# First panel by halves behind X's first tile with 19 zero products ahead; other orders at both attentions' ends and in the last network

## What is computed

```
h = rms_norm(x, g_attn); z = h @ w_in
o_fox = fox_attention(...)                 # 8 heads of 64, causal, with forget gates
o_nsa = nsa_attention(...)                 # 8 heads of 64: compressed, selected and window branches
merged = sigmoid(g_a) * (o_fox @ w_br_fox) + sigmoid(g_b) * (o_nsa @ w_br_nsa)
x = x + merged @ w_out
x = x + square(relu(rms_norm(x, g_mlp) @ w_ff1)) @ w_ff2
x = rms_norm(x, g_final)
...                                        # second block: modulation from c, context keys and values
hx = modulate(rms_norm(x, norm1_g), sh1, sc1)
mix = (sigmoid(g_a) * (attn @ w_attn_out) + sigmoid(g_b) * conformer_conv(u)) @ w_out
x = x + g1 * mix
hx2 = modulate(rms_norm(x, norm2_g), sh2, sc2)
a, b = split(hx2 @ w_up); x = x + g2 * ((gelu(depthwise_conv(a)) * b) @ w_down)
return rms_norm(x, final_g)
```

## Time and profile before

| | |
|---|---|
| median of 3 runs | 1682.06 us (1680.8 to 1686.5) |
| profiled execution, its own time | 1686.16 us |
| its span (first to last instruction) | 1684.4 us |
| PE busy | 1621.0 us (96%) |
| DVE busy | 1110.1 us (66%) |
| ACT busy | 716.3 us (43%) |
| mean granted clock of TensorE | 0.992 |

### The profile page before, as it was taken

The page is one execution under the profiler, slowest core; times in us unless marked ns, Lnnn a source line. Parts: engine busy times, 40 slices in busy tenths (PEclk is TensorE's granted clock), DMA queues, the critical chain, the costliest instruction groups (busy, mean ns, idle before and its releaser), DMA issues.

```text
span 1684.4 us, 21985 instructions
## 1 busy us (share of the span) xinstructions
PE 1621.0 (96%) x7956; PEld 1338.8 (79%) x7956; DVE 1110.1 (66%) x1700; ACT 716.3 (43%) x1236; POOL 164.6 (10%) x188
## 2 busy tenths in 40 slices
PE   7999989989999999999999999999999999999997
PEld 5887777767888888888877787888779888888886
DVE  6666787786676666753686579998765644444446
ACT  5446775665443232322443234545633432232233
POOL 0121200000310000000003970000000000000000
PEclk9999999999999999999999999999999999999999
DMA  4566511112625555532213222221333223322333
GB/s 162 163 180 180 119 47 51 51 59 63 248 89 212 186 191 189 195 125 76 88 63 125 88 63 63 47 61 51 110 109 89 84 92 100 100 93 94 100 100 101
DMA packets 50001, 185.45 MB, mean 110 GB/s; under 512 B 6952, under 2 KB 9256, under 8 KB 47488
## 3 DMA queue, kind: packets, MB, share of 16 engines
q1 hardware_dynamic: 39600, 136.76, 25.6%
q0 software_dynamic: 10320, 47.62, 9.1%
HBM read 174.85 MB, written 6.87 MB: 108 GB/s over the span
## 4 chain that ended last, share of the span: by engine, by line
PE 82%; DVE 10%; ACT 4%; issue 3%; DMA 1%; SPq 0%; ACTq 0%; DVEq 0%
PE ps L2045 18%; PE ps L2047 17%; PE ps L2046 17%; PE ps L2107 2%; PE ps L2109 2%; PE ps L2108 2%; PE ps L2289 1%; PE ps L2454 1%; PE ps L2456 1%; PE ps L2455 1%; PE ps L2291 1%; PE ps L2290 1%; PE ps L2250 1%; PE ps L2511 1%; PE ps L2275 1%
## 5 line engine op out<-in xcount | busy, mean ns | idle before, releaser
L2045 PE MATMUL ps<-h_hi,w_hi 128*128 128x512 f32 x832 | 329.1, 396 | 8.4 <-DVE h_lo L1705 3.7
L2047 PE MATMUL ps<-h_hi,w_lo 128*128 128x512 f32 x832 | 324.0, 389 | 0.0
L2046 PE MATMUL ps<-h_lo,w_hi 128*128 128x512 f32 x832 | 323.9, 389 | 0.0
L1198 DVE TENSOR_TENSOR w_lo<-raw,w_hi 128x1024 fp32r<-128x1024 f32 x181 | 227.6, 1260 | 103.3 <-ACT w_hi L683 77.7
L616 ACT ACTIVATE w_hi<-raw 128x1024 fp32r<-128x1024 f32 x125 | 131.4, 1052 | 166.7 <-DMA raw<-in_panels 166.6
L2045 PEld LDWEIGHTS ps<-h_hi,w_hi 128*128 128x128 f32 x832 | 156.2, 188 | 48.6 <-DVE h_lo L1705 5.8
L2046 PEld LDWEIGHTS ps<-h_lo,w_hi 128*128 128x128 f32 x832 | 156.2, 188 | 33.6 <-issue 1.9
L2047 PEld LDWEIGHTS ps<-h_hi,w_lo 128*128 128x128 f32 x832 | 156.2, 188 | 32.8
L2045 PE MATMUL ps<-f_hi,w_hi 128*128 128x512 f32 x408 | 164.8, 404 | 0.0
L2046 PE MATMUL ps<-f_lo,w_hi 128*128 128x512 f32 x408 | 159.1, 390 | 0.0
L2047 PE MATMUL ps<-f_hi,w_lo 128*128 128x512 f32 x408 | 159.0, 390 | 0.0
(11 more groups left out here) (426 smaller groups left out, 3333.8 us busy)
## 6 DMA issues: line engine op xcount, KB each, us to landing
raw<-in_panels SPq DMA_DIRECT2D x252, 512.0 KB, 3.5
wm<-in_w_mod POOLq DMA_DIRECT2D x16, 1536.0 KB, 8.2
scratch_r<-scratch_t POOLq DMA_DIRECT2D x8, 320.0 KB, 5.3
kd<-k_hi POOLq DMA_DIRECT2D x16, 128.0 KB, 2.6
kd<-k_lo POOLq DMA_DIRECT2D x16, 128.0 KB, 3.3
bias<-scratch_c POOLq DMA_DIRECT2D x8, 256.0 KB, 3.8
bias<-scratch_r POOLq DMA_DIRECT2D x8, 256.0 KB, 3.0
X<-in_x POOLq DMA_DIRECT2D x1, 2048.0 KB, 9.4
```

The lines of the kernel that those rows point to most:

```text
L1198: dve.tensor_tensor(w_lo[:, n % RING], raw[:, n % RING], w_hi[:, n % RING].bitcast(F32), ALU.subtract)\
L2045: pe.matmul(out, w_hi[:, u, b, :], hi[:, k, :N], start=start, stop=False)
L2046: pe.matmul(out, w_hi[:, u, b, :], lo[:, k, :N], start=False, stop=False)
L2047: ins = pe.matmul(out, w_lo[:, u, b, :], hi[:, k, :N], start=False, stop=stop)
```

## The change

1. Start: X's first tile is issued first, then the 8 columns of the vectors that the first norm needs, then panel 0 in two halves of four blocks around X's second tile; the constants come behind panel 1 and the other vectors behind panel 2. ACT and DVE split panel 0 by halves. TensorE begins when the first halves and two tiles of `h_lo` are there. Ahead of it TensorE multiplies a zero tile by itself 19 times into a bank that is not read.
2. `LAST_GATE` names other slots for four gate pieces.
3. `column_sum("norm2", T)` stands ahead of `ctx_part(1)`.
4. Second attention: in steps 14 and later ACT copies part 2 ahead of the exponentials; DVE moves `o2_lo` of head 6 and a tap behind two low parts.
5. Last network: the high and low parts of `up_0`'s panels 1 and 3 come earlier, and the second half's column sum is done in the middle of panel 1.

The semaphore of one table transfer is also merged into `rows_stored`, whose thresholds rise by 16.

```diff
-    LAST_GATE = ((NI - 1, 0), (NI, 2), (NI + 1, 2), (NI + 1, 3))
+    LAST_GATE = ((NI, 2), (NI, 5), (NI + 1, 0), (NI + 1, 2))
...
-        sp.dma_start(vec[:], a["vectors"]).then_inc(in_v, 16)
         for n, (f, g) in enumerate(X_PARTS):
             sp.dma_start(X[:, f:g, :], a["x"][:, f:g, :]).then_inc(in_x[n], 16)
             if n == 0:
-                sp.dma_start(raw[:, 0], a["panels"][0]).then_inc(landed[0], 16)
+                sp.dma_start(vec[:, 0:KT], a["vectors"][:, 0:KT]).then_inc(in_x[0], 16)
+                sp.dma_start(raw[:, 0, 0:4, :], a["panels"][0][:, 0:4, :]).then_inc(sem("first_half_landed"), 16)
+            if n == 1:
+                sp.dma_start(raw[:, 0, 4:8, :], a["panels"][0][:, 4:8, :]).then_inc(landed[0], 16)
+        sp.dma_start(raw[:, 1], a["panels"][1]).then_inc(landed[1], 16)
         sp.dma_start(cst[:, 0:C_EARLY], a["consts"][:, 0:C_EARLY]).then_inc(in_c, 16)
...
# ScalarE, the start
             if f == 0:
-                first_hi(0)
+                act.wait_ge(sem("first_half_landed"), 16)
+                act.activation(w_hi[:, 0, 0:4, :], raw[:, 0, 0:4, :], ACT.Copy)
+            if f == 1:
+                act.wait_ge(landed[0], 16)
+                act.activation(w_hi[:, 0, 4:8, :], raw[:, 0, 4:8, :], ACT.Copy).then_inc(hi_ready, 1)
...
# ScalarE, second attention and last network
-            exp2(w, 0)
-            hi_turn2(w - 1, 2)
+            if w >= UNITS - 2:
+                hi_turn2(w - 1, 2)
+                exp2(w, 0)
+            else:
+                exp2(w, 0)
+                hi_turn2(w - 1, 2)
...
+        panel_hi(BASE["up_0"] + 1)
         second_square("out2", "norm_ffn", 6)
-        panel_hi(BASE["up_0"] + 1)
...
# VectorE, second attention
-            taps_at(w, 0)
+            taps_at(w, 0) if w < UNITS else None
             lo_turn2(w - 1, 0)
             lo_turn2(w - 1, 1)
+            if w == UNITS:
+                o2_lo(H2 - 2)
+                taps_at(w, 0)
...
-            if w >= 3 and w % 2:
+            if w >= 3 and w % 2 and w != UNITS - 1:
                 o2_lo((w - 3) // 2)
...
# VectorE, last network
         ffn_low(0, 6)
+        panel_lo(BASE["up_0"] + 1)
         ffn_low(0, 7)
...
-        panel_lo(BASE["up_0"] + 1)
+        panel_lo(BASE["up_0"] + 2)
         inverse("norm_ffn", 1)
-        panel_lo(BASE["up_0"] + 2)
+        panel_lo(BASE["up_0"] + 3)
...
         for f in range(1, KT):
-            if f == 2:
-                panel_lo(BASE["up_0"] + 3)
...
# TensorE
-            pe.wait_ge(lo_ready, n + 1)
+            pe.wait_ge(lo_ready, n + 1) if n else None
...
-                    pe.wait_ge(n_lo, k + 1)
+                    pe.wait_ge(n_lo, max(k, 1) + 1)
+                if n == 0 and k == 4:
+                    pe.wait_ge(lo_ready, 1)
...
+        pe.wait_ge(setup, 1)
+        zeros = p_cmp[0][:].rearrange("p t c -> p (t c)")
+        for n in range(19):
+            pe.matmul(ps[:, 7, 0:P], zeros, zeros, start=True, stop=True)
...
         ctx_part(0)
+        column_sum("norm2", T)
         ctx_part(1)
-        column_sum("norm2", T)
...
-            half_panel(BASE["up_0"] + m, m, 0, ready=(lambda k: (n_lo, 24 + k + 1)) if m == 0 else None)
-            half_sum("norm_ffn", 1) if m == 0 else None
+            half_panel(BASE["up_0"] + m, m, 0, ready=(lambda k: (n_lo, 24 + k + 1)) if m == 0 else None,
+                       at_four=(lambda: half_sum("norm_ffn", 1)) if m == 1 else None)
```

More of the change, by code:

```diff
@@ L468, in _ @@
             if n == 0:
-                sp.dma_start(raw[:, 0], a["panels"][0]).then_inc(landed[0], 16)
+                sp.dma_start(vec[:, 0:KT], a["vectors"][:, 0:KT]).then_inc(in_x[0], 16)
[3 more added lines that the diff above has]
+        sp.dma_start(raw[:, 1], a["panels"][1]).then_inc(landed[1], 16)
         sp.dma_start(cst[:, 0:C_EARLY], a["consts"][:, 0:C_EARLY]).then_inc(in_c, 16)
-        for u in range(1, RING):
-            sp.dma_start(raw[:, u], a["panels"][u]).then_inc(landed[u], 16)
+        sp.dma_start(raw[:, 2], a["panels"][2]).then_inc(landed[2], 16)
+        sp.dma_start(vec[:, KT:V_ALL], a["vectors"][:, KT:V_ALL]).then_inc(in_v, 16)
+        sp.dma_start(raw[:, 3], a["panels"][3]).then_inc(landed[3], 16)
         if total > RING:
@@ L494, in _ @@
         gp.wait_ge(sem("rel_rows"), 2)
-        gp.dma_start(scratch_t, r8[:]).then_inc(sem("rel_placed"), 16)
-        gp.wait_ge(sem("rel_placed"), 16)
+        gp.dma_start(scratch_t, r8[:]).then_inc(sem("rows_stored"), 16)
+        gp.wait_ge(sem("rows_stored"), 16)
         for n in range(8):
@@ L537, in _ @@
         gp.dma_start(w2v[:], a["w2v"]).then_inc(sem("w2_loaded"), 16)
-        gp.wait_ge(sem("rows_stored"), 16)
+        gp.wait_ge(sem("rows_stored"), 32)
         bias_rows(0)
@@ L595, in _ @@
             gp.dma_start(scratch_f[h], factor[:, h % 2, :]).then_inc(sem("rows_stored"), 16)
-            gp.wait_ge(sem("rows_stored"), 16 * (h + 2))
+            gp.wait_ge(sem("rows_stored"), 16 * (h + 3))
             gp.wait_ge(sem("factor_loaded"), 16 * h) if h else None
@@ L701, in _ @@
         act.activation(row_max[:, 0, 0:1], p_cmp[0][:, 0, 0:1], ACT.Copy)
-        act.wait_ge(in_v, 16)
         for f in range(KT):
-            act.wait_ge(in_x[X_PART_OF[f]], 16)
+            act.wait_ge(in_x[X_PART_OF[f]], 16 if f else 32)
             act.activation(h_hi[:, f, :], X[:, f, :], ACT.Copy, scale=vcol("g_attn", f)).then_inc(n_hi, 1)
             if f == 0:
-                first_hi(0)
+                act.wait_ge(sem("first_half_landed"), 16)
[3 more added lines that the diff above has]
+                act.activation(w_hi[:, 0, 4:8, :], raw[:, 0, 4:8, :], ACT.Copy).then_inc(hi_ready, 1)
         first_hi(1)
@@ L715, in _ @@
         act.wait_ge(in_c, 16)
+        act.wait_ge(in_v, 16)
         act.activation(row_max[:, 0, 0:1], eps, ACT.Sqrt)
@@ L1206, in _ @@
         dve.memset(blk_f[:].rearrange("p j (g c) -> p (j g) c", c=CW)[:, :, NCB:CW], 0.0).then_inc(setup, 1)
-        dve.wait_ge(in_v, 16)
+        dve.wait_ge(in_x[0], 32)
         for f in range(KT):
             dve.wait_ge(n_hi, f + 1)
+            if f == 1:
+                dve.tensor_tensor(w_lo[:, 0, 0:4, :], raw[:, 0, 0:4, :], w_hi[:, 0, 0:4, :].bitcast(F32), ALU.subtract)
             dve.scalar_tensor_tensor(h_lo[:, f, :], X[:, f, :], vcol("g_attn", f), h_hi[:, f, :].bitcast(F32),
                                      ALU.mult, ALU.subtract).then_inc(n_lo, 1)
-            if f == 0:
-                panel_lo(0)
+            if f == 1:
+                dve.wait_ge(hi_ready, 1)
+                dve.tensor_tensor(w_lo[:, 0, 4:8, :], raw[:, 0, 4:8, :], w_hi[:, 0, 4:8, :].bitcast(F32), ALU.subtract)\
+                   .then_inc(lo_ready, 1)
         panel_lo(1)
@@ L1224, in _ @@
         panel_lo(3)
+        dve.wait_ge(in_v, 16)
         dve.wait_ge(n_rms, 1)
@@ L1820, in factor2_of @@
             dve.wait_ge(sem("exp2_done"), 2 * (w + 1))
-            dve.wait_ge(sem("rows_stored"), 16 * h) if h >= 2 else None
+            dve.wait_ge(sem("rows_stored"), 16 * (h + 1)) if h >= 2 else None
             dve.reciprocal(factor[:, h % 2, :], row_sum[:, h % 2, :]).then_inc(sem("o_factor"), 1)
```

## The result

The changed kernel takes 1674.95 us (median of 8 executions, 1672.59 to 1678.14); the kernel before took 1683.89 us in its 8 executions beside them (1680.8 to 1686.5). The ratio is 0.9949, with a 95% interval of 0.9938 to 0.9960: 8.6 us faster by the ratio, 8.9 by the two medians. Forecast were 1672.5 in a range of 1668 to 1680, and "faster" with 0.77. The profiled execution took 1677.28 us (span 1675.5, mean granted clock 0.992), 8.9 less than that of before.

The account below looks back on a forecast made before the run. TensorE's stream plus its waits and slow stretches bound the kernel. -2.8 + 0.3 - 1.6 - 4.0 - 3.1 = -11.2; with 1.6 taken off for clock, 9.6 below 1682.06 is 1672.5 us, range 1668 to 1680.

Parts of the forecast that it names:

- Start: Up to panel 1's first product: TensorE begins it at 15.4 instead of 18.25, a gain of 2.8 us.
- the bound of 15: At the start, worst case: the zero products end near 15 us and the start loses 3.
- First attention's end: Moving gate pieces around the last unit's turns costs 0.3 us; bounds: gain of 0.8, loss of 1.5.
- Norm 2: Column sum moved ahead: TensorE waits 0.6 for it, the reciprocal starts at 853.6 instead of 855.22; gain 1.6 us.
- Second attention's end: Reordering on DVE (1.3 us) and ACT (1.1) shortens TensorE's wait, and the clock stays up (1.6); gain 4.0 in sum.
- the third: Second attention's end: with a shorter wait the clock should not fall, giving back 1.7 us, counted as 1.6.
- rival E: Inside the two attentions, short waits bring the clock down more often; 1.7 us per stretch, 1689.5 with ten; chance 0.04.
- Last network: Panel 1's products fill the column sum's wait and the last `h_lo` ends earlier; `up_0`'s second round gains 3.1 us.
- new stretches: Sign against the prediction: the clock shows new stretches at 0.50 inside the attentions.
- 1.6 off for clock in a lump: Whole kernel: 1.6 us of the gain taken off for stretches at 0.50 that a median run did not have.
- rivals B: Clock still falls at the second attention's end and for longer in the last network; gain 6.4, 1675.7 us; chance 0.18.
- C: Start gives 0.5 instead of 2.8 us, since X's and panel 1's landings don't move and cutting costs; 1674.8; chance 0.10.

## Why the prediction was right, and by how much

**Start: right, 0.3 too large.** The order of events was as told: zero products, then fast real ones, then a short wait for panel 1's low part (0.25). The sizes behind it: panel 1's high part began at 13.23, where I had put 13.0, and the low part ended at 15.56 for 15.35; the first real product came at 9.03 for 8.5, since the zero products ended at 8.89 and tile 1's low part at 8.98 (tile 1 came at 6.87 and not 6.3). Of the 2.5, the zero products carry 1.3, shown by taking them out; their end at 8.9 is far from the bound of 15. The 4 KB of vector columns did hold the first `h_hi` back: the trace's landing events have X's tile at 3.16 and the columns at 3.58, 0.4 later, where the prediction had 0.7; `h_hi` of tile 2 waited for a later landing, as told. The Trainium skill (DMA: Bandwidth & Descriptors, Bandwidth) gives 0.68 us as the time that the DMA engines are busy with 4 KB. No run here shows that time; the 0.4 is the distance of two landings, another measure.

**First attention's end: +0.3 forecast, 0.0 found.** The two changes cancel as I had reckoned, only more closely. Slot (32, 0), which the change doesn't use, stands right ahead of the wait of 1.9, and a piece there fills it; what that is worth, 0.4 to 0.7 in the profiles, the executions do not show.

**Norm 2: right.** -1.3 to -1.7 in the twelve profiles with the new order, -1.5 in that of the changed kernel, and 0.0 in the one without it. That one takes back four parts at once, so this rests on the place and not on a run of its own. The sum waited 0.52 for 0.6; the reciprocal stands at 851.48, which is 853.74 with the 2.26 gained up to there, for 853.6.

**Second attention's end: sum right (-3.8 for -4.0), and the parts too.** VectorE 1.3 for 1.3, ScalarE 0.95 for 1.1. The step that was mis-stated is the third: 1.6 for a clock that no longer falls. The stretch was there in the one profiled execution of before and in none of the three other profiles with the old order, though they waited 2.5 us in full. It is a gain against that execution, not against most of the profiles. It was also sized right only for this place: the stretch there cost 1.6, but one costs 0.7 to 1.2 at the others where it can be read off (at 1309 in before, 297 and 1014 in the changed kernel), and 1.0 by the executions, not the 1.7 that the prediction counts per stretch in rival E.

**Last network: right, 0.5 too large (-2.6 for -3.1).** The column sum stands without a wait. The last `h_lo` ends at 1315.51, which is 1321.8 with the 6.26 gained before, for 1321.7; what I left out is the 0.3 us between the last half-panel and `up_0`'s second round (0.16 of it is the idle time in the earlier trace rows). The 2.9 us per half-panel is what the trace has, 24 products 0.12 apart; from half of 0.229 it would be 2.7.

**What the sum did not have.** The five terms were 10.4 instead of 11.2, and 1.5 was given back outside them: the stretches at 0.50 inside the two attentions cost 2.5 more than before, and the reload of X, on which a wait of 1.06 hung in before's trace, gave 1.1. The prediction named new stretches as what would prove it wrong, and they came; rival E was thus right in kind and small in size. Its reading of the clock was off: the 27 us at 0.50 that the mean of 0.992 gives do not contain the start, as the prediction has it, but 20.5 us between 179 and 1317 us and 6.4 at the very end.

I had taken 1.6 off for clock in a lump, as a thing of the profiled execution. The forecast of the gain, 9.6, came close to the 8.9 of the medians, and this is in part luck: what took the profile's 11.2 down to 8.9 was 0.8 of terms too large and 2.5 of stretches at new places, less the 1.1 at the reload of X, and not a stretch that a median run lacks. Of the 2.5 us by which 1672.5 missed the median, 1.8 is the median of before, 1682.06 over 3 runs and 1683.89 over 8. The time alone would also fit rivals B (1675.7) and C (1674.8). The profile decides against both: nothing at 0.50 behind 1018 while TensorE works, and 2.5 gained at the start.
